# Attention probabilities of two query tiles of four turned in 32x32 blocks on VectorE and set in place through DRAM, instead of by TensorE

## What is computed

```python
def block_attention(q, k, v):          # 16 heads, 512 queries, 768 keys (256 context + 512 tokens)
    s = jnp.einsum('bqhd,bkhd->bhqk', qblk, k).astype(F32) * scale    # qblk: 128 queries of q
    p = jax.nn.softmax(s, axis=-1).astype(v.dtype)
    return jnp.einsum('bhqk,bkhd->bqhd', p, v)
```

## Time and profile before

| what | value |
| --- | --- |
| median of 3 runs | 1645.06 us |
| lowest, highest run | 1644.56 us, 1647.28 us |
| profiled execution, span | 1645.5 us |
| TensorE busy | 1633.9 us, 99% of the span |
| VectorE, ScalarE, GpSimd busy | 1043.6, 571.0, 1026.5 us |
| mean granted TensorE clock | 0.997 of full |

### The profile page before, as it was taken

One profiled execution on the slowest core, in us unless ns is written; L12 is line 12 of the kernel. 1 busy time (PEld: TensorE's weight loads), 2 busy tenths in 40 slices (PEclk: granted clock), 3 DMA queues, 4 the chain that ended last, 5 costly groups with the idle time before them and its releaser, 6 DMA issues.

```text
span 1645.5 us, 24018 instructions
## 1 busy us (share of the span) xinstructions
PE 1633.9 (99%) x8950; PEld 1364.2 (83%) x8950; DVE 1043.6 (63%) x1537; ACT 571.0 (35%) x1017; POOL 1026.5 (62%) x656
## 2 busy tenths in 40 slices
PE   9999999999999999999999999999999999999998
PEld 7887778798888888889887798888888898888887
DVE  3567777677877865635487566655558359746173
ACT  3467777633233232203344243222222121123111
POOL 3455766656666766575579456666676645567663
PEclk9999999999999999999999999999999999999999
DMA  9234335232269863435322233344434253223332
GB/s 371 87 90 129 111 106 165 79 93 96 89 211 320 298 225 103 141 137 172 120 90 65 77 99 102 125 156 140 153 106 143 97 214 120 65 84 103 91 101 90
DMA packets 59095, 220.61 MB, mean 134 GB/s; under 512 B 6849, under 2 KB 9153, under 8 KB 55682
## 3 DMA queue, kind: packets, MB, share of 16 engines
q1 hardware_dynamic: 53826, 204.96, 38.2%
q10 hardware_dynamic: 5184, 14.49, 2.3%
HBM read 201.07 MB, written 14.16 MB: 131 GB/s over the span
## 4 chain that ended last, share of the span: by engine, by line
PE 95%; DVE 4%; ACT 0%; issue 0%; DMA 0%; DVEq 0%; SPq 0%; ACTq 0%
PE PS L2444 28%; PE PS L2446 28%; PE PS L2445 28%; PE PS L2821 3%; PE PS L2783 2%; PE PS L1012 1%; PE PS L2430 1%; PE PS L1785 1%; PE PS L2595 1%; DVE SC L3572 0%; DVE WA L1990 0%; PE PS L1791 0%; DVE MR L3522 0%; PE PS L2720 0%; PE PS L2721 0%
## 5 line engine op out<-in xcount | busy, mean ns | idle before, releaser
L2354 POOL TENSOR_TENSOR WL<-RAW,WH 128x1024 fp32r<-128x1024 f32 (+3 forms) x211 | 542.8, 2572 | 17.6
L2444 PE MATMUL PS<-HH,WH 128*128 128x512 f32 (+1 forms) x1340 | 507.5, 379 | 0.0
L2446 PE MATMUL PS<-HH,WL 128*128 128x512 f32 (+1 forms) x1340 | 502.9, 375 | 0.0
L2445 PE MATMUL PS<-HL,WH 128*128 128x512 f32 (+1 forms) x1340 | 502.9, 375 | 0.0
L2351 POOL TENSOR_SCALAR WH<-RAW 128x1024 fp32r<-128x1024 f32 (+3 forms) x211 | 239.4, 1134 | 287.8 <-PE PS L2446 276.5
L2444 PEld LDWEIGHTS PS<-HH,WH 128*128 128x128 f32 x1340 | 252.2, 188 | 50.7 <-issue 6.2
L2446 PEld LDWEIGHTS PS<-HH,WL 128*128 128x128 f32 x1340 | 252.2, 188 | 45.9
L2445 PEld LDWEIGHTS PS<-HL,WH 128*128 128x128 f32 x1340 | 252.3, 188 | 43.9
L2379 POOL TENSOR_SCALAR PR<-PR,SC 128x768 f32<-128x768 f32 x47 | 107.3, 2292 | 66.7 <-DVE SC L3579 66.3
L2444 PE MATMUL PS<-HIDH,WH 128*128 128x512 f32 (+1 forms) x396 | 145.3, 367 | 0.0
L2445 PE MATMUL PS<-HIDL,WH 128*128 128x512 f32 (+1 forms) x396 | 144.8, 366 | 0.0
(11 more groups left out here) (532 smaller groups left out, 2894.6 us busy)
## 6 DMA issues: line engine op xcount, KB each, us to landing
RAW<-in_wup SPq DMA_DIRECT2D x88, 512.0 KB, 3.6
MRF<-in_modw SPq DMA_DIRECT2D x52, 512.0 KB, 4.8
RAW<-in_wdn SPq DMA_DIRECT2D x32, 704.0 KB, 4.1
MR<-in_modw SPq DMA_DIRECT2D x28, 512.0 KB, 3.6
RAW<-in_whin SPq DMA_DIRECT2D x24, 512.0 KB, 3.5
MK<-in_modk SPq DMA_DIRECT2D x8, 1024.0 KB, 10.9
RAW<-in_wo SPq DMA_DIRECT2D x8, 512.0 KB, 4.2
hy_hs<-HST ACTq DMA_DIRECT2D x4, 1024.0 KB, 4.0
```

The costliest lines, as they stand in the source:

```text
L2354: pool.tensor_tensor(WL[s][:, 0:n], raw[:, 0:n], WH[s][:, 0:n].bitcast(F32), ALU.subtract).then_inc(tile_split, 1)
L2444: pe.matmul(out, wh, xh, start=first, stop=False)
L2445: pe.matmul(out, wh, xl, start=False, stop=False)
L2446: return pe.matmul(out, wl, xh, start=False, stop=last)
```

## The change

With `BLOCKED = 2`, the query tiles 0 and 1 of each head go another way:

- ScalarE writes their exponentials in another order of columns: where key = 128 t + 32 c + j, the column is 192 c + 32 t + j.
- After GpSimd has normalised them, VectorE turns each [128, 768] tile in place in 32x32 blocks (`block_turn`), one instruction a tile.
- SP stores each tile to DRAM (`blocks_out`, 384 KB) and, when both stores have landed and `value(h-1)` is done, issues 8 loads of 96 KB (`blocks_in`), each of which takes 32 DRAM rows as 4 x 32 x 192 elements and lays them on 128 partitions of PB. There is one buffer PB.
- TensorE turns only the query tiles 2 and 3: 12 blocks a head in three groups of four, with three copies by ScalarE. `value(h)` reads queries 0 to 255 from PB and 256 to 511 from PT.
- The modulation rows are placed anew: 8 (`PRE_ROWS`) are done by VectorE between the maxima and reciprocals of head 0, 2 in head 0, 2 in each odd head from 1 to 11, 3 in heads 13 and 14.
- Loops on the SP queue are written out, the second load of X comes behind the last head, and several semaphores are merged or renamed (`uvp` and `latent` to `low_rank`, `xadd` to `sq_add`, `ctx_in` and `tab_in` to `side_in`), with their thresholds moved accordingly.

```diff
+            def blocks_out(h, qt):
+                sp.wait_ge(S["turned"], BLOCKED * h + qt + 1)
+                sp.dma_start(d_blocks[h % 2, :, qt, :], PR[h % 2][:, qt, :]).then_inc(S["blocks_out"], 16)
+
+            def blocks_in(h):
+                sp.wait_ge(S["pv"], h + 1)
+                sp.wait_ge(S["blocks_out"], 16 * BLOCKED * (h + 1))
+                for qt in range(BLOCKED):
+                    for m in range(4):
+                        sp.dma_start(PB[:, m, qt, :, :].rearrange("p t j -> p (t j)"),
+                                     d_blocks[h % 2, 32 * m:32 * m + 32, qt, :].rearrange("k (c x) -> c k x", c=4)
+                                     ).then_inc(S["blocks_in"], 16)
...
+            for r in range(PRE_ROWS + 2):
+                mod_load(16 + r)
+                if r == 1:
+                    head_weights(2)
...
+            for h in range(16):
+                if h % 2 and h < 11:
+                    head_weights(h // 2 + 3)
+                elif h == 11 or h == 13:
+                    ring("wo", a["wo"], h // 2 - 5)
+                if h > 12:
+                    for r in range(3 * h - 17, min(3 * h - 14, EARLY)):
+                        mod_load(16 + r)
+                elif h % 2:
+                    mod_load(16 + PRE_ROWS + 1 + h)
+                    mod_load(16 + PRE_ROWS + 2 + h)
+                if h % 4 == 3 and h < 12:
+                    rope_move(h + 1, 2)
+                elif h % 4 == 0 and 0 < h < 13:
+                    rope_move(h + 2, 2)
...
+                for qt in range(BLOCKED):
+                    blocks_out(h, qt)
+                blocks_in(h)
+            x_again(1)
```

On TensorE, ScalarE and VectorE:

```diff
+                for kt in (2 * n, 2 * n + 1):
+                    for qt in range(BLOCKED, 4):
+                        q = (kt % 2) * 256 + (qt - BLOCKED) * P
+                        m = pe.transpose(PS[:, 6 + n % 2, q:q + P], PR[h % 2][:, qt, kt * P:(kt + 1) * P], IDENT[:, :])
...
+                pe.wait_ge(S["blocks_in"], 16 * 4 * BLOCKED * (h + 1))
                 for kt in range(6):
-                    pe.wait_ge(S["pt"], 7 * h + kt + 2)
-                    for half in range(2):
-                        m = pe.matmul(PS[VH * half:VH * half + VH, out_bank(h), 0:256], V[:, kt, v],
-                                      PT[:, kt, tok(half)], start=kt == 0, stop=kt == 5)
+                    pe.wait_ge(S["pt"], 4 * h + kt // 2 + 2)
+                    pe.matmul(PS[0:VH, out_bank(h), 0:256].rearrange("p (i m j) -> p i m j", i=2, m=4), V[:, kt, v],
+                              PB[:, :, :, kt, :].rearrange("p m i j -> p i m j"), start=kt == 0, stop=kt == 5)
+                    m = pe.matmul(PS[VH:2 * VH, out_bank(h), 0:256], V[:, kt, v], PT[:, kt, :], start=kt == 0, stop=kt == 5)
...
+                if qt < BLOCKED:
+                    out, src = out.rearrange("p (c t j) -> p t c j", c=4, t=6), src.rearrange("p (t c j) -> p t c j", t=6, c=4)
...
+            def block_turn(h, qt, i=0, per=0):
+                dve.wait_ge(S["pnorm"], i * (3 * per) + (3 * h + qt if h else qt + 1))
+                dve.transpose(PR[h % 2][:, qt, :], PR[h % 2][:, qt, :]).then_inc(S["turned"], 1)
...
+                if h < 15:
+                    block_turn(h + 1, 0, i, per)
                 if h % 2:
                     row(1)
+                if h in (13, 14):
+                    row(2)
+                if h < 15:
+                    block_turn(h + 1, 1, i, per)
                 out_lo(h, i, per)
...
             maximum(0, 0)
+            pre_rows(0, 1)
             maximum(0, 1)
             inverse_sum(0, 0)
+            pre_rows(1, 2)
             inverse_sum(0, 1)
             maximum(0, 2)
+            pre_rows(2, 4)
             maximum(0, 3)
             inverse_sum(0, 2)
+            pre_rows(4, 6)
             inverse_sum(0, 3)
-            head(0, range(0, 2))
+            pre_rows(6, 8)
+            for qt in range(BLOCKED):
+                block_turn(0, qt)
+            head(0)
```

More of the change, by code:

```diff
@@ L46 @@
 EARLY, LATE, LAST_ROWS = 28, 11, 88
+BLOCKED = 2
+PRE_ROWS = 8
 EPS = 1e-6
@@ L2243, in _, with x_again @@
             rope_move(2, 2)
[L2244 to L2259, removed]
+            for r in range(PRE_ROWS + 2):
+                mod_load(16 + r)
+                if r == 1:
+                    head_weights(2)
+            def x_again(k):
                 sp.wait_ge(S["s_ready"], 56 + 8 * k)
                 sp.dma_start(X[:, 4 * k:4 * k + 4, :], a["x"][:, 4 * k:4 * k + 4, :]).then_inc(S[f"x_in{k}"], 16)
+            for h in range(16):
[13 more added lines that the diff above has]
+                    rope_move(h + 2, 2)
+                elif h == 14:
+                    sp.wait_ge(S["rope"], 512)
+                    x_again(0)
+                for qt in range(BLOCKED):
+                    blocks_out(h, qt)
+                blocks_in(h)
+            x_again(1)
             with sp.Fori(0, 3) as i:
@@ L2778, in score, with turn @@
                 m.then_inc(S["s_ready"], 1)
[L2780 to L2800, removed]
+            def turn(h, n):
+                if n == 0:
                     pe.wait_ge(S["pnorm"], 3 * h + 2)
@@ L2836, in head @@
             def head(h):
[L2838 to L2842, removed]
+                turn(h, 0)
+                turn(h, 1)
                 for qt in range(4):
@@ L2861, in head @@
                         wo_ahead(1, qt // 2)
-                    turn(h, qt + 2)
+                    if qt == 1:
+                        turn(h, 2)
                 if h < 14 and h % 2 == 0:
@@ L3589, in out_lo, with head @@
                                       ALU.subtract).then_inc(S["olo"], 1)
-            def head(h, rows, i=0, per=0):
+            def block_turn(h, qt, i=0, per=0):
+                dve.wait_ge(S["pnorm"], i * (3 * per) + (3 * h + qt if h else qt + 1))
+                dve.transpose(PR[h % 2][:, qt, :], PR[h % 2][:, qt, :]).then_inc(S["turned"], 1)
+            def head(h, i=0, per=0):
                 def row(k):
-                    if rows:
-                        if k == 0 and h % 2 == 0 and h:
-                            dve.wait_ge(S["modx"], i * (per // 2) + h // 2)
-                        mod_rows(rows[k], i, 2 * per, MACC[:, rows[k] % 4:rows[k] % 4 + 1], MR, CB[:, :])
+                    if h == 0:
+                        r = PRE_ROWS + k
+                    elif h == 15:
+                        return
+                    elif h > 12:
+                        r = PRE_ROWS + 3 * (h - 13) + 14 + k
+                    elif h % 2:
+                        r = PRE_ROWS + 2 + h - 1 + k
+                    else:
+                        return
+                    if per:
+                        if h == 1 and k == 0:
+                            dve.wait_ge(S["modx"], i + 1)
+                        mod_row(r, MACC[:, r - PRE_ROWS - 2:r - PRE_ROWS - 1], i, per)
+                    else:
+                        mod_row(r, MOD[:, 16 + r:17 + r])
                 late_row = h % 4 == 0 and 0 < h <= 12
@@ L3606, in head @@
                     inverse_sum(h + 1, 0, i, per)
-                    row(0)
                     maximum(h + 1, 2, i, per)
@@ L3610, in head @@
                     query_lo(h + 2, i, per)
-                    row(1)
                     maximum(h + 1, 3, i, per)
```

110 lines of the change are left out of this document (61 added, 49 removed).

## The result

The changed kernel takes 1774.95 us (median of 4 runs, 1773.5 to 1779.68), the kernel before 1646.17 beside it (1644.56 to 1647.37): a ratio of 1.0788 [1.0771, 1.0805], 129 us slower, where 87 was forecast. That lies in the stated range, 5 us under its upper end (1780), and outside the forecast's own 1715 to 1755. The profiled execution spans 1774.1 us.

What follows compares the result with a forecast made beforehand. TensorE, busy 99%, bounds the kernel before; block delivery then paces it. Value products start at 138.4, plus 17.0 and seven pairs totalling 245.7, reach 401.1, 87.0 late: 1732 us, own range 1715 to 1755, stated range 1660 to 1780.

Steps and rivals of the forecast that it cites:

- R2: Rival: block loads on four engines, each packet costing 50 ns whatever its size; 1762 to 1777 us, chance 0.14.
- Step 1: On TensorE, 12 of 24 turns go in each of 16 heads: 20.9 us saved, 1.3 us a head.
- V(0): Head 0's value product on TensorE: forecast at 138.4 us, 13.4 late.
- V(15): Head 15's value product on TensorE: forecast at 401.1 us against 314.09, later by 87.0.
- R3: Rival: all 16 engines carry the block loads; still slower, 1657 to 1667 us, chance 0.10.
- R4: Rival: not slower if an odd head's blocks land under 3.5 us after release; 1630 to 1648 us, chance 0.06.
- Step 2: Eight rows on VectorE ahead of head 0 cost about 9 us; head 1's first maximum 9.5 us late.
- Step 3: Blocks' way through DRAM: store 2.4 us, eight loads on four engines landing 11.5 us after release.
- B: Time from release to landing of a head's eight block loads: 11.5 us, to 14.8.
- Step 4: Delivery against TensorE: one PB buffer sets at least 14.3 us between value products, the source 19.0 or 18.3.
- Step 5: TensorE's clock halves for 7 us after each odd-head stall: 3.5 us of work lost, buffer limit becomes 17.0.
- R1: Rival: block loads on four engines, TensorE's clock stays up; pair of heads 31.7 us, 1706 us, chance 0.20.

Runs made afterwards that it cites:

- e12: e11 without VectorE's block turns of heads 1 to 15: 1663.8 us, ratio 1.0105.
- e4: The kernel before with only the modulation rows placed anew, eight ahead of head 0: 1658.17 us, ratio 1.0071.
- e7: e6 with four block loads of 192 KB a head instead of eight of 96 KB, blocks ordered differently in DRAM and PB: 1696.6 us.
- e8: e7 with both block turns right behind the last reciprocal and the second row's load behind blocks_in: 1680.82 us.
- e1: The changed kernel with block loads cut by destination group, so that they run on all 16 DMA engines: 1706.42 us, ratio 1.0372.
- e2: The changed kernel with the third row of heads 13 and 14 loaded behind blocks_in instead of ahead of the stores: 1760.1 us.
- e3: The changed kernel with 24 extra 128x128 matmuls a head on TensorE ahead of its wait for the blocks: 1770.78 us.
- e6: e1 with the modulation rows placed as before the change: 1690.16 us, ratio 1.0275.
- e11: The changed kernel with blocks stored and loaded for head 0 only, later heads reading those: 1677.81 us, ratio 1.0191.
- e9: e8 with tile 0's turn moved behind the maximum of tile 2 and tile 1's behind that of tile 3: 1670.1 us.
- e10: e9 with four block loads of 96 KB for each tile, issued as soon as that tile's store has landed: 1670.11 us.

## Why the prediction was right, and where not

The direction, the mechanism (V to V set by the delivery of the blocks) and the four engines held, and the time lies in the range, near its end. The size, 43 us short, is the sum of misses of both signs. The measured 1775 is the time of R2 (1762 to 1777), but by luck: R2 wanted 50 ns for a packet of 768 bytes, and it took 38. By its steps:

- **Step 1** counted rightly 192 turns fewer, but its 21 us are not to be had: e12, with VectorE's turns and the moves of 15 heads away, is 17 us slower than before. In its trace V(0) is 19.1 us late (11.6 of it the rows, by e4, and 7.5 head 0's delivery), and only 6 us come back up to V(15). As soon as TensorE has 1.3 us less a head, VectorE's and ScalarE's chain of maximum, exponential and reciprocal is late next. The step took TensorE's work as the only pace, although show VectorE waiting now for TensorE, now for ScalarE. In the forecast itself this hardly counted, as the delivery stood above it; it spoils R3 and R4.
- **Step 2** came out (head 1's first maximum was forecast 9.5 us late, and is 10.1: 125.10 against 115.04), in part by luck: SP is free sooner than taken, the first row ends at 103.4 instead of 106.3, and two rows then cost 5.4 to 7.3 us instead of 5.0. VectorE's timeline of the changed kernel, the first and last rows and what follows:

```profile
102.24 1.23 DVE L3547 CUSTOM_DVE_ANT_0 MR<-MR,CB 128x1024 f32<-128x1024 f32 x1 [5.07 <-DMA MR<-in_modw]
...
118.61 3.65 DVE L3547 CUSTOM_DVE_ANT_0 MR<-MR,CB 128x1024 f32<-128x1024 f32 x1 [1.65 <-DMA MR<-in_modw]
...
123.34 1.83 DVE L3619 STREAM_TRANSPOSE PR<-PR 128x768 f32<-128x768 f32 x2
125.10 0.92 DVE L3597 TENSOR_REDUCE SC<-PS 128x1 f32<-128x768 f32 x1
```

  A turn took 0.96 us (0.9 taken). Alone, the rows cost 12 us (e4).
- **Step 3** had the engines and the packet right (4; 38 ns for 37). Mis-sized are two terms. A store takes 4.5 us, not 2.4, with 7.6 in head 3. And B, from the first issue to the value product, is 12.6 us on average. It is 11.1 and 11.2 in heads 1 and 5, behind whose loads SP issues nothing for 5 us, and 11.2 in head 14, near the 11.5 of the sum. In ten others, nearly all with weights, rows or moves issued right behind the loads, it is 12.3 to 12.8, and in heads 7, 9 and 13, where the eight issues took SP 7 to 8 us instead of 6, 13.4 to 14.6. Both terms were priced by loads and stores that ran alone, while step 4 says itself that what queues on SP beside them is left out. That omission is the step that failed first. For the store it is shown, for B it is read from these heads only. e7 to e8, where the row's load between the stores goes (and the turns move), takes 2.0 us off a store's landing, and e1 shows the other direction, rows 2.6 us later behind slow loads.
- **Step 4** forecast 35.1 us for a pair of heads. Measured from V(1): 39.3, 33.8, 40.3, 36.6, 39.0, 45.7, 47.0, together 281.8 for 245.7. The ordinary pairs fit; the pairs with heads 3, 7 and 11, ahead of whose stores weights, rows and moves of queries are issued, have 4 to 5 us more each; the last two have the third rows, 15 us by e2, a wait that the step did not list.
- **Step 5** saw the clock rightly (0.69 to 0.83 in the windows above, 0.84 over 125 to 400 us) and probably priced it too high. R1 differs from the forecast by it alone, 26 us; against that stand the 4 of e3, which are net of its filling, and the 15 of the estimate beside it, which is for one path. So 22 us at most stood there too many, 11 by the estimate, and with the 40 us by which V(15) was missed, the other terms were short by 51 to 62. Of the sizes above, an estimate makes that 51: in nine heads the loads' issue follows the landing of the stores, 9 x 2.1 = 19; 1.1 us of B in 16 heads are 17; and the third rows 15.
- **R3** had its mechanism confirmed by e1 and its time 40 us too low (its own terms add up to 1665 at the upper end, not 1667). V(0) of e1 is 5 us later than R3 had it (138.8 for 133.5). What else stood there the experiments show by what moving it gave, which is not its share of the 40: the rows and the third rows 16 (e6), the turns with the second row's load 16 (e8), the turns once more 10 (e9). Step 1's saving was not there either.
- **R4** asked for a delivery under 3.5 us. e11 takes the delivery away for 15 heads and is 32 us slower. Less the 8.5 of head 0's delivery it would, by an estimate, still be 23 slower, of which the rows are 12: no speed of the moves alone would have made this change pay.

What stays open: why four loads are slower than eight (e7); what the clock costs without a filling; and what ScalarE's strided order adds, which no run takes apart. No version with the turned blocks beats the kernel before. Of those that deliver them for every head, e9 and e10 come nearest, at 1.4% over it.

## What to carry to other kernels

A move through DRAM cost more here by what shared its queue than by its own bytes: list what the issuing engine's queue holds ahead of each link, and price a transfer by its neighbours in that queue, not by a row where it ran alone. When work is taken from the engine that is busy 99%, ask first how much shorter than its period the chain of waits between the other engines is: here that left 6 of 20 us. And before a clock that falls in a wait is charged in full, see in which stages the slow stretch releases the next one: here it was 7 of 16. And matmuls that are to keep the clock up cost their own time wherever the wait is shorter than they are.

## What was not expected of the hardware

A store of 384 KB that takes 2.4 us alone landed in 7.6 where block loads on four engines, a weight load, two row loads of 512 KB and four moves had been issued ahead of it on the same queue. With the loads over 16 engines (e1) the stores of that head landed in 4.5 us by the median of the two, instead of 6.2. The Trainium skill ("DMA: Bandwidth & Descriptors", the HWDGE ordering part of its queue model) says that one issuer's copies share one ring on each DMA engine and are consumed in ring order; the rise, and its vanishing in e8, agree. A copy over four engines took SP 536 ns to issue, the same bytes over 16 engines 432, by the medians above; the pattern of the copy changed with it.

The seventh row ahead of head 1 took VectorE 3.65 us instead of 1.23, and 3.60 to 3.92 in e1, e4, e11 and e12. Each time GpSimd's product of 128x1280 had begun up to 0.5 us before it, and the row ended 1.1 us behind GpSimd's end. GpSimd's timeline of the changed kernel, where the row ran from 118.61 to 122.26:

```profile
118.24 2.94 POOL L2386 TENSOR_TENSOR WL<-RAW,WH 128x1280 fp32r<-128x1280 f32 x1
```

In e2 a row began 0.14 us before GpSimd's product and took 1.23 us, and the product 3.90. In both orders the instruction that began second ended late; no run takes the cause apart. The fifth row, 2.18 us, looks the same (GpSimd's product of 128x768 ends at 113.91, the row at 114.99). Together they are 3.4 us of step 2.
